# One decode step of a sparse-attention and MoE layer: routing inside the output product, earlier lists, gathers and weights, other waits

## The reference

```python
def merge_and_channel_mix(x, attn_out, gm_out, ga, gb, w_branch_a, w_branch_b, w_o, ...):
    merged = ga * (attn_out @ w_branch_a) + gb * (gm_out @ w_branch_b)
    h = layer_norm(DEEPNORM_ALPHA * x + merged @ w_o, ln1_g, ln1_b)
    f = hierarchical_moe(h, ...)
    return layer_norm(DEEPNORM_ALPHA * h + f, ln2_g, ln2_b)

def hierarchical_moe(x, ...):
    lg = xt @ w_router_group + b_router_group            # 4 groups
    gsel = argmax(lg); pg = softmax(lg)[gsel]
    le = xt @ w_router_expert + b_router_expert          # 8 experts in each group
    vals, eidx = top_k(le[gsel], 2)
    pw = softmax(vals) * pg
    # each row: sum over its two experts of pw * (silu(x @ gate) * (x @ up)) @ down
```

## Time and profile before

| | us |
|---|---|
| median of 3 runs | 1455.95 |
| profiled execution, own time | 1466.36 |
| its span, first to last instruction | 1464.9 |
| PE busy | 1353.8 (92%) |
| PE weight load | 696.5 (48%) |
| DVE busy | 705.2 (48%) |
| ACT busy | 281.8 (19%) |
| POOL busy | 238.8 (16%) |

### The profile page before, as it was taken

How to read it: one execution, slowest core, us unless ns; L and a number is a source line. 1 busy time by engine, 2 the same in 40 slices (tenths; PEclk the granted TensorE clock), 3 DMA queues, 4 the chain that set the end, 5 groups by cost and what they waited for, 6 DMA issues and landing times. The chain is left out here.

```text
span 1464.9 us, 19047 instructions
## 1 busy us (share of the span) xinstructions
PE 1353.8 (92%) x6651; PEld 696.5 (48%) x6651; DVE 705.2 (48%) x1657; ACT 281.8 (19%) x624; POOL 238.8 (16%) x292
## 2 busy tenths in 40 slices
PE   7999999799999999999898889899964999999985
PEld 2444444345466666666566656355531333333321
DVE  0211123498988888984544944456671111111135
ACT  0100112322321111111554420000000111111124
POOL 3121000042320000110243100001111111111113
PEclk9999999899999999999899989999986999999998
DMA  9311002210032111110232139511116899999935
GB/s 315 89 58 49 16 16 73 80 56 1 0 107 71 65 65 65 69 61 35 83 95 65 58 120 356 227 29 29 29 29 267 328 408 407 403 411 412 411 157 227
DMA packets 70475, 213.98 MB, mean 146 GB/s; under 512 B 16603, under 2 KB 42203, under 8 KB 60026
## 3 DMA queue, kind: packets, MB, share of 16 engines
q1 hardware_dynamic: 56426, 184.60, 33.7%
q0 software_dynamic: 12688, 27.76, 5.6%
q10 hardware_dynamic: 1280, 0.53, 0.2%
HBM read 186.33 MB, written 34.65 MB: 151 GB/s over the span
## 5 line engine op out<-in xcount | busy, mean ns | idle before, releaser
L238 PE MATMUL ps_mixer<-front,x_all 128*128 128x512 f32 (+1 forms) x448 | 180.4, 557 | 1.7 <-ACT wi L382 1.7
L927 DVE TENSOR_SCALAR_CACHE_REDUCE front<-score,bound 128x384 bf16<-128x384 f32 (+2 forms) x198 | 174.0, 940 | 0.4 <-DVE bound L949 0.3
L1849 PE MATMUL main_ps_experts<-w_gate_up,main_e_rowsT 128*32 128x512 f32 (+1 forms) x1280 | 172.0, 601 | 1.6 <-DVE main_e_rowsT L1957 1.6
L238 PEld LDWEIGHTS ps_mixer<-front,x_all 128*128 128x128 f32 x448 | 83.2, 190 | 91.7 <-issue 81.2
L1558 PE MATMUL ps_merge<-w_o,mergedT 128*128 128x512 f32 x256 | 113.5, 602 | 3.0 <-DVE h_rows L1697 3.0
L755 PE MATMUL ps_mixer<-x_all,front 128*128 128x344 f32 x384 | 114.4, 453 | 0.0
L755 PE MATMUL ps_mixer<-x_all,w_gate 128*128 128x344 f32 x384 | 113.3, 453 | 0.0
L1849 PEld LDWEIGHTS main_ps_experts<-w_gate_up,main_e_rowsT 128*32 128x32 f32 (+1 forms) x1280 | 50.3, 116 | 106.1 <-issue 106.1
L1962 DVE TENSOR_TENSOR main_hidden<-main_hidden,main_ps_experts 128x256 f32<-128x256 f32 x24 | 10.1, 421 | 173.9 <-ACT main_hidden L1909 173.9
L755 PEld LDWEIGHTS ps_mixer<-x_all,w_gate 128*128 128x128 f32 x384 | 72.7, 190 | 37.5
L755 PEld LDWEIGHTS ps_mixer<-x_all,front 128*128 128x128 f32 x384 | 72.6, 190 | 37.1
(11 more groups left out here) (304 smaller groups left out, 1673.6 us busy)
## 6 DMA issues: line engine op xcount, KB each, us to landing
w_gate_up<-in_w_gate_up SPq DMA_DIRECT2D x32, 2048.0 KB, 13.9
w_down<-in_w_down SPq DMA_DIRECT2D x32, 1024.0 KB, 10.2
w_gate_up<-pair_out SPq DMA_DIRECT2D x8, 1024.0 KB, 13.9
front<-in_w_qkvi SPq DMA_DIRECT2D x8, 930.0 KB, 18.9
w_gate<-in_w_gate SPq DMA_DIRECT2D x4, 1280.0 KB
front<-in_w_gate SPq DMA_DIRECT2D x4, 1280.0 KB
h_rows<-in_x_rows SPq DMA_DIRECT2D x9, 512.0 KB, 5.9
h<-h_rows SPq DMA_DIRECT2D x18, 256.0 KB
```

The costliest lines, as they stand in the source:

```text
L238: mm = nc.tensor.matmul(ps[:, g % 2, 0:c1 - c0], x_all[:, k, t * P:(t + 1) * P], w[:, k, c0:c1], start=(k == 0), stop=(k == KC - 1))
L927: V.tensor_scalar(waste[0:n, at - width:at], s, column(bound, g), None, compare, ALU.add, accum_out=column(number, g)).then_inc(taken, 1)
L1849: mm = nc.tensor.matmul(ps[c0:c1, GU, :], rowsT[j][:, k, c0:c1], w_gu[b][:, k, :], start=(k == 0), stop=(k == KC - 1))
```

## The change

- **First loads.** `x_few` is an input of its own. The first 1024 columns of weight block 0 (512 KB) and the k = 0 part of x tile 0 (64 KB) come first with semaphores of their own, and PE starts with the first two column groups.
- **make_few_uv.** The first half of its steps stands ahead of the last turn.
- **Gathers.** Each of 24 units issues two gathers (K, K; own K and V's first half; V's second half and own V), where it was 2, 3 and 1, and each waits for a copy on PE's side of the last chunk of its unit (`wait_for_turn`).
- **Routing.** It works on the raw rows: DVE folds LN1's gain into the router's weights (`w_fold`) after unit 16, PE sums their columns, and DVE makes logits = (product - mean * column sum) * rstd + bias. Turn, route, turn_logits and rank of tile i-1 stand between matmuls of `project(i)`, whose results have two pairs of PSUM banks. ACT normalises the row in place, POOL multiplies by LN1's gain and adds its bias. `place(i-1)` stands between the two halves' adds of tile i.
- **End of the block.** List load, `tokens`, the softmax weights and the first two row gathers stand in merge_and_route. W_AHEAD is 3. The expert block's row, hidden and result buffers live in the memory of `w_o`.
- **Finish.** Four tiles are grown before the pair rows are there, then `grow(t+3)` behind tile t. The wait for y's stores stands after the branch.

```diff
-                pe.wait_ge(x_in[0], 16)
+                pe.wait_ge(few_in, 16)
+                pe.wait_ge(w_first_in, 16)
+                first_few(0, (0, 1))
+                pe.wait_ge(x_first_in, 16)
+                first_rows(0, (0, 1))
+                pe.wait_ge(w_in[0], 16)
+                first_few(0, (2, 3))
+                first_rows(0, (2, 3))
+                pe.wait_ge(x_in[0], 16)
...
+            def wait_for_turn(n):
+                wait_copied(pool, chunk_of[n, 1, units[n][0] // 4 * 4])
...
             for b in range(N_SAMPLE):
-                pool.wait_ge(masked, 2 * (N_SAMPLE + b) + 1)
+                wait_for_turn(N_SAMPLE + b)
                 gather_own(k_of, "k_all", b, k_in)
-                gather(v_of, "cache_v", b, v_in)
-            pool.wait_ge(v_in, 32 * N_SAMPLE)
+                gather(v_of, "cache_v", b, 0, v_in)
+            pool.wait_ge(v_in, 16 * N_SAMPLE)
             for b in range(N_SAMPLE):
-                pool.wait_ge(masked, 2 * (2 * N_SAMPLE + b) + 1)
+                wait_for_turn(2 * N_SAMPLE + b)
+                gather(v_of, "cache_v", b, 1, v_in)
                 gather_own(v_of, "v_all", b, v_in)
...
+                if n == FOLD_AT:
+                    dve.wait_ge(w_r_in, 16)
+                    dve.wait_ge(const_in, 16 * N_CONST)
+                    for which in range(2):
+                        nc.vector.tensor_tensor(w_fold[:, :, which, :], w_r[:], ln1_t[:, which, :]..., ALU.mult)
...
+                        if at == TURN_AT:
+                            turn(i - 1)
+                        if at == ROUTE_AT:
+                            route(i - 1)
+                        if at == LOGITS_AT:
+                            turn_logits(i - 1)
+                        if at == RANK_AT:
+                            rank(i - 1)
+                        mm = nc.tensor.matmul(ps[:, PROJECTED[i % 2][c], :], mergedT[:, k, t * P:(t + 1) * P],
...
# POOL, per tile
+                nc.gpsimd.tensor_scalar(minus_mean[i % 2], mv[i % 2][:, 0:1], var, -1.0, ALU.mult, ALU.mult)
+                pool.wait_ge(normed, i + 1)
+                nc.gpsimd.tensor_tensor(h[:, t, :], h[:, t, :], ln1[:, 0, :], ALU.mult).then_inc(gained, 1)
+                pool.wait_ge(gained, i + 1)
+                nc.gpsimd.tensor_tensor(h[:, t, :], h[:, t, :], ln1[:, 1, :], ALU.add).then_inc(h_ready, 1)
+                pool.wait_ge(slots_ready, i + 1)
+                for which in range(2):
+                    pool.indirect_dma_start(...)                       # scatter to list_of
+            pool.wait_ge(tokens_ready, 1)
+            pool.wait_ge(h_out, 32 * TILES)
+            for e in range(2):
+                gather_rows(pool, scratch, keep["e_rows"][e], tokens, e, keep["rows_in"][e])
...
# ACT, per tile
+                act.wait_ge(minus_ready, t + 1)
+                nc.scalar.activation(hb, hb, ACT.Identity, bias=minus_mean[t % 2], scale=mv[t % 2][:, 1:2])
...
# DVE, per tile
+                    add(i, 0)
+                    place(i - 1)
+                    add(i, 1)
+                step(V.bn_aggr(mean[:], ...))
+                V.tensor_scalar(mean[:, 1:2], mean[:, 1:2], EPS, None, ALU.add).then_inc(measured, 1)
+                read_logits(i)
+                pick(i)
...
-W_AHEAD = 2
+W_AHEAD = 3
...
             for e in range(loaded, W_BUFS):
+                if e >= 2:
+                    sp.wait_ge(rows_in[e - 2], 16)
                 load_gate_up(e)
                 load_down(e)
...
             pe.wait_ge(spread_ready, 1)
-            grow(1)
+            for t in range(1, 4):
+                grow(t)
...
-                if t + 2 < NT:
-                    grow(t + 2)
+                if t >= 1 and t + 3 < NT:
+                    grow(t + 3)
...
-            sp.wait_ge(y_out, 16 * (TILES + 1))
+        wait_for_y(nc.sync, keep, "first")
```

More of the change, by code:

```diff
@@ L350, in _ @@
                         score_dots(unit_at[t, g])
+            make_few_uv(range(0, KC // 2))
             turn(NT - 1)
@@ L353, in _ @@
                 score_dots(n)
-                make_few_uv(range(0, KC // 2) if n < len(units) - 1 else range(KC // 2, KC))
+                make_few_uv(range(KC // 2, KC - 2) if n < len(units) - 1 else range(KC - 2, KC))
         @block.scalar
@@ L1110, in _ @@
             wait_for_gates_stored(pool)
+            def wait_for_turn(n):
+                wait_copied(pool, chunk_of[n, 1, units[n][0] // 4 * 4])
             for b in range(N_SAMPLE):
-                pool.wait_ge(masked, 2 * b + 1)
-                gather(k_of, "cache_k", b, k_in)
+                wait_for_turn(b)
+                for half in range(2):
+                    gather(k_of, "cache_k", b, half, k_in)
             pool.wait_ge(own_ready, 1)
@@ L1428, in merge_and_route @@
         both = free[4:6]
+        after = FREE + 10 * N_EXPERTS + 2 * ROUTER
+        e4 = over[:, after:after + TILES * N_GROUPS].rearrange("p (t g) -> p t g", g=N_GROUPS)
+        e2, sum_g, den = (over[:, after + TILES * (N_GROUPS + n):after + TILES * (N_GROUPS + n + 1)] for n in range(3))
+        most = over[:, after + TILES * (N_GROUPS + 3):after + TILES * (N_GROUPS + 3) + 1]
+        minus_mean = [over[:, after + TILES * (N_GROUPS + 4) + j:after + TILES * (N_GROUPS + 4) + j + 1] for j in range(2)]
+        tokens, entries = (keep[n][:, 0:PACKS] for n in ("tokens", "entries"))
+        minus_sum, part = (over[:, FREE + 10 * N_EXPERTS + n * ROUTER:FREE + 10 * N_EXPERTS + (n + 1) * ROUTER] for n in range(2))
         share, lin, address, wrap = free[6].bitcast(I32), free[7], free[8], free[9]
@@ new lines, in measure, with add_few @@
+            def measure(i, c):
+                step(V.bn_stats(stats[:, c, :], h[:, tiles[i], c * 512:(c + 1) * 512]), wait=(c == 1))
+            def add_few():
+                t = tiles[0]
+                dve.wait_ge(projected, 1)
+                dve.wait_ge(x_in[0], 16)
+                for late in range(2):
+                    for c in range(2):
+                        few = h[0:FEW, t, c * 512:(c + 1) * 512]
+                        g = 2 * late + c
+                        V.scalar_tensor_tensor(few, few, 1.0 if late else ALPHA, ps[g * FEW:(g + 1) * FEW, 0, :],
+                                               ALU.mult, ALU.add).then_inc(added, 1)
+                    dve.wait_ge(added, 2 + 2 * late)
+                measure(0, 0)
+                measure(0, 1)
@@ new lines, in add, with read_logits @@
+            def add(i, c):
+                dve.wait_ge(projected, 2 * i + c)
+                dve.wait_ge(x_in[i], 16)
+                half = h[:, tiles[i], c * 512:(c + 1) * 512]
+                V.scalar_tensor_tensor(half, half, ALPHA, ps[:, PROJECTED[i % 2][c], :], ALU.mult, ALU.add).then_inc(added, 1)
+                dve.wait_ge(added, 4 + 2 * i - 1 + c)
+                measure(i, c)
+            def read_logits(i):
+                mean = mv[i % 2]
+                dve.wait_ge(powed, i + 1)
+                dve.wait_ge(lg_turned, i + 1)
+                V.scalar_tensor_tensor(part, minus_sum, mean[:, 0:1], ps[:, ROUTED, P:P + ROUTER],
+                                       ALU.mult, ALU.add).then_inc(logits_read, 1)
+                dve.wait_ge(logits_read, i + 1)
+                step(V.scalar_tensor_tensor(logits[:, tiles[i], :], part, mean[:, 1:2], b_r[:], ALU.mult, ALU.add))
@@ new lines, in _ @@
+            place(TILES - 1)
+            w = keep["weights"]
+            V.tensor_tensor(e4, logits[:, :, 0:N_GROUPS], best_g.unsqueeze(2).to_broadcast([P, TILES, N_GROUPS]),
+                            ALU.subtract).then_inc(exp_ready, 1)
+            V.tensor_tensor(e2, best2, best1, ALU.subtract).then_inc(exp_ready, 1)
+            dve.wait_ge(counted, 1)
+            step(V.tensor_reduce(most, ps[:, TURNED[1], 0:N_EXPERTS], AX.X, ALU.max))
+            step(V.tensor_copy(keep["most"][:], most[0:1, :]))
@@ L1762, in experts @@
         stored = [sem(f"e_stored{j}") for j in range(2)]
-        weighed = sem("weighed")
         if loaded:
-            last = Finish(nc, outs, keep, scratch, sb, "first", ps, [rows[j][:] for j in range(2)])
+            last = Finish(nc, outs, keep, scratch, sb, "first", ps, rows)
         block = ctx.enter_context(nc.Block())
@@ L2153, in finish_again @@
         ps = ctx.enter_context(nc.psum_tensor("ps_again", [P, 8, 512], F32))
-        last = Finish(nc, outs, keep, scratch, sb, "again", ps, [sb(f"z{j}", [P, D])[:] for j in range(2)])
+        last = Finish(nc, outs, keep, scratch, sb, "again", ps, keep["e_rows"])
         h_in = nc.alloc_semaphore("h_again_in")
@@ L2180, in _ @@
         def _(dve):
+            last.vector_grown(dve)
             last.vector_spread(dve)
```

340 lines of the change are left out of this document (184 added, 156 removed).

## The result

The changed kernel takes 1434.89 us, the median of four runs (1433.4 to 1442.77), against 1456.38 of before (1453.18 to 1457.12, four runs). The ratio is 0.9874, 95% interval 0.985 to 0.9899: 15 to 22 us faster. The forecast was 32 us. The two profiled executions, 1466.36 and 1435.39, are 31 us apart, close to the forecast; so it is the profiled execution of before that stands 10 us off the others, and the first question is which stage holds them.

A forecast was written before the change was run, and what follows sets the result against it. PE was taken as the bound, with gains from its waits or low-clock work. Terms sum to -31.9 against the profiled 1466.36: 1434.5, times 0.993 gives 1424 us; own range 1416 to 1431, 8 in 10 range 1412 to 1436.

The forecast's parts named there:

- the attention's -8.5: Attention: with two gathers in every unit, PE's 8.7 us of waits on probsT go; -8.5 us (+3 to -12).
- the tail's -15.5: Last project's end (E) to first expert matmul: earlier slots and early row gathers shorten 44.07 us; -15.5 (-12 to -18).
- Rival 1: Attention: gathers cost by number, not grouping, so waits only move to other units; 8.5 us stays, 1432.5 us, chance 0.14.
- Start, -2.6: Kernel start: smaller first loads bring the first matmul from 8.67 to 6.2 us; -2.6 us (0 to -4).
- make_few_uv, 0 (-2 to 0): Steps ahead of the last turn: they fill a PE wait in a stage ending with DVE's scoring; 0 us (-2 to 0).
- Merge, +1.0: Merge ahead of routing: extra small loads, two DVE multiplies and eight narrow PE matmuls cost +1.0 us (0 to +2.5).
- Routing loop, -2.5: Project and routing tiles: filled PE waits cut the cycle from 18.21 to 17.48 us, less a held pick; -2.5 (-4.7 to +33).
- Rival 4: Routing loop: POOL's two 128x1024 operations and DVE's pick lock each other in every tile; +40 us, 1463 us, chance 0.04.
- Expert phase, 0: Expert matmuls: a missing expert's weights are made up while buffers fill; 0 us (0 to +10).
- Rival 2: Expert phase: PE waits for weights or rows at some packs; +6.5 us, 1431 us, chance 0.10.
- Finish, -3.5: Finish: two of six grown tiles move ahead of the pair sums, into an existing wait; -3.5 us (-2 to -5.5).
- y wait, -0.3: End of kernel: the wait for y's stores moves behind the last branch; -0.3 us (0 to -1.5).

The follow-up runs named there:

- three gathers: Changed kernel with the old gather grouping and trigger (2, 3 and 1 a unit): 0.9873 of before on the first chip; 1449.24 us, 0.987 on the fourth.
- third late: Changed kernel with the third expert's weights loaded at the start of the expert block, behind the first row gather: 1439.12 us, 0.9791 of before.
- gain in the gap: Changed kernel with LN1's gain and bias moved from POOL to DVE, while DVE waits for the next tile's logits: 1433.23 us, 0.9755 of before.
- gap late: Changed kernel with LN1's gain and bias in DVE's wait for logits and the first two row gathers back in the expert block: 1432.23 us, 0.9748.

## Why the prediction was right and wrong

- **Which step failed.** Two terms of the sum. The first is the attention's -8.5, with the time against which it was summed. The prediction took all 10.4 us between the profiled execution and the median as a factor of 0.993 spread over everything. Against the profile of a 1453 us chip 10.9 us stand in the attention (160.0 and 149.1) and 3.1 in the routing loop (151.1 and 148.0, at a granted clock of 0.98 and 1.00). The term was read from rows that the executions behind the median most likely did not have, and there it measured 0. The second is the tail's -15.5, which measured -10.9 and -11.0 in the two pairs of the table; its wrong steps are named below. On the chip of 1469 us on which both were timed the change brings 30 us (0.9796), on the first chip, of 1453, it brings 16, and 21 in the first result. That 30 is near the forecast 32 is luck: from the profile of before on the fourth chip to that of the changed kernel on the third the attention gives 12.5 in place of 8.5 and the tail 12.0 in place of 15.5. Of the rivals the first has the nearest number (1432.5 for 1434.89), but not by its mechanism.
- **Its own sign.** The prediction called itself wrong as a whole if attention and loop together gave nothing. On the first chip they are 197.1 before (149.1+148.0) and 197.9 after: nothing.
- **Attention, -8.5 (+3 to -12).** Right in kind where the waits exist, and too small there (13 on the fourth chip, for the cold matmuls behind the waits go as well), 0 on the first chip. Rival 1 (the number counts, not the grouping) is wrong: 48 gathers are issued in both, and on the fourth chip the waits went.
- **Start, -2.6.** The first matmul came at 5.93 and PE did not wait again in the first blocks (forecast 6.2). 45 us in, 2.2 of it are there, at the attention nothing. In the changed kernel's two profiles the granted clock drops once, to 0.89 (45 to 60 us) in one and 0.95 (180 to 210 us) in the other, about 1.7 us each; the second profile of before shows 1.00 in these windows. But the drop is not the whole answer. Four profiles with the same start (three gathers on the first chip, third late, gain in the gap, gap late) have a clock of 1.00 up to 270 us, and their next block still starts at 288.9 to 290.3, where before has 289.4 and 290.0. In these only 0.6 to 1.7 us of the gain are left 46 us in, because the low clock at the start lasts longer: x tile 0's first four matmuls take 3.78 in all four, 2.63 and 3.00 in the changed kernel's two. Some 0.4 us of the rest go in the next point.
- **make_few_uv, 0 (-2 to 0).** The wait of 5.64 became 3.80 and two waits of 0.7 to 0.9 for the weights of the half that stayed. They stand ahead of a product of scores, on which DVE waits: from the end of the longer wait to the next block's first matmul it takes 15.0 us in both profiles of the changed kernel, 14.7 and 14.5 in those of before. So the part costs some 0.4 us instead of nothing.
- **Merge, +1.0.** 65.2 and 65.5 before, 65.6 and 67.5 after: inside the forecast (0 to 2.5). Ten further profiles of changed kernels have 64.4 to 65.4, so the cost is nearer 0.
- **Routing loop, -2.5.** The loop takes 148.8 in each profile of the changed kernel, 148.6 was forecast. The cycle is 17.8 us instead of 17.48, by the 0.3 that a held pick costs. But the 151.1 of before is not what it always takes: 148.0, 149.7 and 152.7 in its later profiles, with cycles of 18.21 in all four and a granted clock of 0.98, 1.00, 0.99 and 0.97. Against the 148.0, at the same clock of 1.00 as the changed kernel's, the term is +0.8: the cycles do get shorter, but one routing more lies inside the loop, and the first cycle takes 19.34. Its mechanism was right; that POOL's operation stops a two-input DVE operation for as long as it lasts, and not by tenths, the trace of before did show, two rows further on than the one that was read. The same line of POOL as in the earlier trace rows, 0.91 in most of its 24 instructions, took 2.98 beside a DVE operation of 2.34 with two inputs that had started 0.13 ahead of it, and ended 0.77 behind that one's end:

```profile
633.68 2.34 DVE L965 SCALAR_TENSOR_TENSOR score_s<-score_s,bound,front 8x2049 f32<-8x2049 f32 x1
```

```profile
633.81 2.98 POOL L909 TENSOR_TENSOR front<-front 128x344 f32<-128x344 f32 x1 [15.28 <-ACT front L869]
```

The rule cited (the Trainium skill, "SBUF — State Buffer", "SBUF: two separate sides") is borne out by these and by the 1.62 and 2.16 us rows. The hold costs here 3 to 4 us in the loop and 2.8 on the last slots. Rival 4 needed every operation of the pick to be caught; one is in each of the first eight tiles (router_logits, 1.3 to 2.3 us) and two in the last, since POOL's work ends.
- **Tail, -15.5 (-12 to -18): -10.9.** Two steps failed. Slots came at E+16.8, forecast 12.6 to 15.8: one us later than the case with a low clock, though the clock held; without POOL's two operations they come at E+14.0. The block boundary took 5.7 to 6.3, not 3.85: two gathers are in flight when the block ends, and without them it is 2.6 from the tokens, not 9.5. Both ends were named; the middle was the wrong choice. PE's first expert matmul came at E+33.2, later than the E+32 of the worst case.
- **Expert phase, 0.** -0.9 and +1.6, 0 within what it varies. Rival 2 is out: PE has no wait for weights, not even with the third expert loaded late, and for rows it has none over 1.0 us in the profiles of the changed kernel.
- **Finish, -3.5.** -5.0, and +4.4 when undone. The prediction priced the two grown tiles at 1.98 each; the one behind the first sum still runs at the low clock and takes 2.85 before, so the two give 4.8. The sums themselves give 0.3 (5.35 for two against 3.68 and 1.94), so the first still runs cold. ACT stays behind PE by 1.16 as before. The stage ahead, in which four tiles are now grown, ends 0.7 to 0.9 later, which leaves about 4.1.

```profile
1424.73 2.85 PE L2050 MATMUL main_ps_experts<-h_rows,main_f_grown 128*128 128x512 f32 x4
```

- **y wait, -0.3.** The rest of the span is 15.2 and 15.4 against 14.8 and 15.2: nothing won that these profiles show.

With 0 for the attention, 0 for the start, +0.8 for the loop, -11 for the tail and -5 for the finish the sum is -15.2, against -16.0 between the medians on the first chip (1453.26 to 1437.27). That is less of a check than it looks: the merge, the experts and the two short stages are left out, and they are +4.5 in that pair, whose profiles are 10.5 us apart. The profile of the changed kernel there is the longest of its six executions, which spread from 1433.34 to 1442.22 with a granted clock of 0.978 to 0.970.

## What to carry to other kernels

When the profiled execution is 0.7% off the median of its own runs, look for the stage that holds the difference before any row of it is priced; waits that stand in four of eight like units are the first suspect. Work moved from VectorE to GpSimd was not free where VectorE had a two-input operation in the meantime: the place for it here was VectorE's own idle gap, 5.9 us faster than the changed kernel (with the gathers late too it is the fastest version run, but not by more than the executions vary). Row gathers in flight at the end of a block were paid at the boundary. And a sum that comes out right is worth little until each of its terms has been measured.

## What the runs showed that I had not expected

- The same kernel takes 1453 us on two chips and 1469 on two others, at clocks of 0.968 and 0.963. In one profile of each kind 12 us of the difference stand in the attention, with its waits behind three gathers in a row, and 5 ahead of it (703.0 and 697.7).
- A DVE operation on 128x4 elements took 2.16 us beside a POOL operation of 2.34, and ended with it; a reduction with one input in the same stretch took 0.16, an operation with one of its inputs in PSUM 0.25.
- The block boundary takes 5.7 to 6.3 us from the last of two row gathers' issue, and 7.0 us separate the last scatter from the first gather where the list is read in between and no gather is in flight; the gathers' own landing (1090.28 for the one issued at 1084.78) is 1.8 us ahead of the expert block's start.
- A start 2.7 us earlier was used up before 300 us: by a longer stretch at the low clock at the start or a drop of 1.7 us later on, and by the weights of make_few_uv. With neither drop nor early start (whole loads) the next block starts at the same 289.8.
- The last scatter's landing, on which the list waits, came 1.7 us later when the stores of the last tile's rows were issued beside it.
